# Norm weights applied ahead of the projections, the root behind them, in a two-layer hybrid block on one core

## The reference

```
h = rmsnorm(x, norm1_g);  P = h @ w_in            # four parts: rwkv, dsa, retention, gates
merged = sum over 3 branches of sigmoid(gate) * (y_branch @ w_branch)
x = x + merged @ w_o
h2 = rmsnorm(x, norm2_g)
x = x + square(relu(h2 @ w_up)) @ w_down          # d_ff = 4096
rmsnorm(x, g) = x * rsqrt(mean(x*x) + 1e-6) * g
```

## Time and profile before

| | |
|---|---|
| median of three runs | 2961.14 us (2960.81 to 2964.19) |
| profiled execution | 2957.23 us, of which 2955.4 us is the span of the profile |
| busy: PE, DVE, ACT, POOL | 91%, 44%, 19%, 35% of the span |

### The profile page before, as it was taken

One profiled execution on the slowest core, in us unless ns is written; L12 is line 12 of the kernel. 1 busy time (PEld: TensorE's weight loads), 2 busy tenths in 40 slices (PEclk: granted clock), 3 DMA queues, 4 the chain that ended last, 5 costly groups with the idle time before them and its releaser, 6 DMA issues.

```text
span 2955.4 us, 61291 instructions
## 1 busy us (share of the span) xinstructions
PE 2691.1 (91%) x24862; PEld 2460.6 (83%) x24862; DVE 1309.7 (44%) x2092; ACT 575.8 (19%) x1233; POOL 1032.4 (35%) x596
## 2 busy tenths in 40 slices
PE   7978899599998999999989789995999989999997
PEld 6877688389887989999988678874998789899997
DVE  3245885433337442332252468844343363522332
ACT  2112223411212120110111112233121211200111
POOL 3502232011223545555533033320222245455553
PEclk9979899699999999999999799986999999999999
DMA  4201112111133312222232111111111343222221
GB/s 169 87 28 62 42 58 71 57 46 48 51 120 116 122 59 85 85 79 84 85 106 73 36 58 47 61 64 46 58 51 54 120 135 98 65 86 79 84 85 53
DMA packets 64552, 222.53 MB, mean 75 GB/s; under 512 B 7888, under 2 KB 8656, under 8 KB 63056
## 3 DMA queue, kind: packets, MB, share of 16 engines
q1 hardware_dynamic: 43200, 158.23, 16.8%
q10 hardware_dynamic: 21136, 61.17, 5.9%
HBM read 190.34 MB, written 29.03 MB: 74 GB/s over the span
## 4 chain that ended last, share of the span: by engine, by line
PE 79%; DVE 10%; DVEq 5%; issue 3%; ACT 2%; ACTq 1%; DMA 0%
PE dense L460 62%; PE mix L460 15%; DVEq L1348 5%; ACT region_b L934 1%; DVE region_b L1528 1%; DVE region_b L1582 1%; PE mix L837 1%; DVE region_b L1584 1%; DVE region_a L1367 1%; DVE in_lo L1701 0%; DVE region_b L1641 0%; DVE region_b L1595 0%; DVE x L1563 0%; PE mix L535 0%; DMA x<-in_x 0%
## 5 line engine op out<-in xcount | busy, mean ns | idle before, releaser
L460 PE MATMUL dense<-act_hi,w_hi 128*128 128x288 f32 x3296 | 969.8, 309 | 40.0 <-DVE act_lo L1360 29.0
L444 POOL TENSOR_SCALAR w_hi<-w_raw 128x1024 fp32r<-128x1024 f32 x296 | 312.5, 1056 | 1865.6 <-PE dense L460 1502.8
L460 PE MATMUL dense<-act_lo,w_hi 128*128 128x288 f32 x3296 | 929.7, 297 | 0.0
L447 POOL TENSOR_TENSOR w_lo<-w_raw,w_hi 128x1024 fp32r<-128x1024 f32 x296 | 719.8, 2432 | 24.7
L460 PEld LDWEIGHTS dense<-act_hi,w_hi 128*128 128x128 f32 x3296 | 626.9, 190 | 103.8 <-issue 49.2
L460 PE MATMUL dense<-act_hi,w_lo 128*128 128x288 f32 x3296 | 707.3, 296 | 0.0
L460 PEld LDWEIGHTS dense<-act_lo,w_hi 128*128 128x128 f32 x3296 | 628.4, 191 | 0.0
L460 PEld LDWEIGHTS dense<-act_hi,w_lo 128*128 128x128 f32 x3296 | 534.5, 190 | 0.0
L460 PE MATMUL dense<-in_hi,w_hi 128*128 128x288 f32 x1408 | 399.0, 297 | 23.9 <-DVE y_mix L1710 12.6
L460 PE MATMUL dense<-in_lo,w_hi 128*128 128x288 f32 x1408 | 398.4, 298 | 0.0
L460 PE MATMUL dense<-in_hi,w_lo 128*128 128x288 f32 x1408 | 304.8, 298 | 0.0
(11 more groups left out here) (180 smaller groups left out, 2583.5 us busy)
## 6 DMA issues: line engine op xcount, KB each, us to landing
w_raw<-in_stream SPq DMA_DIRECT2D x296, 512.0 KB, 3.5
y_mix<-gate_scratch ACTq DMA_DIRECT2D x48, 288.0 KB, 2.8
gate_scratch<-region_b ACTq DMA_DIRECT2D x36, 288.0 KB, 2.1
x_scratch<-x ACTq DMA_DIRECT2D x2, 2304.0 KB, 8.9
y_scratch<-y_mix ACTq DMA_DIRECT2D x2, 2304.0 KB, 8.0
x<-x_scratch ACTq DMA_DIRECT2D x2, 2304.0 KB, 10.0
y_mix<-y_scratch ACTq DMA_DIRECT2D x2, 2304.0 KB, 9.5
gate_scratch<-region_a ACTq DMA_DIRECT2D x12, 288.0 KB, 2.1
```

What stands on the lines that cost most here:

```text
L444: nc.gpsimd.tensor_scalar(w_hi[:, v, :], w_raw[:, s, :], 1.0, 1.0, ALU.mult, ALU.mult).then_inc(w_high, 1)
L447: nc.gpsimd.tensor_tensor(w_lo[:, v, :], w_raw[:, s, :], w_hi[:, v, :].bitcast(F32), ALU.subtract).then_inc(w_split, 1)
L460: return nc.tensor.matmul(out, lhsT, rhs, start=start, stop=stop, skip_group_check=True)
```

## The change

The norm weight is taken into the operand at once, and the root is multiplied onto what leaves PSUM: `(x*g*r) @ W = ((x*g) @ W) * r`, with r per token.

- ACT squares a column tile and right behind it writes the high part of x times the weight; DVE writes the low part (`low_part`) and adds up the squares (`sum_square`). PE does the first tile behind a norm as its slices come, and only then the sum, of two products instead of eight (`sum_squares` stands behind tile 0).
- Behind w_in the root goes onto whatever reads PSUM: the rotary tables (multiplied by the root once a layer, two multiplications of 128 x 1152), v and gates of retention, dsa's v and index weights, the RWKV tiles (`shift_raws`, now on DVE, in the step in which the tile is finished, with ACT making mu times the row before), and the 24 gates as they come back from DRAM (`scale_gate`). In the MLP DVE does relu times root, ACT square and rounding.
- The roundings of the branch inputs and of the merged results go from DVE to ACT. x is loaded, and y stored, in 8 pieces.
- in_hi and in_lo grow from 12 to 16 tiles, so that MLP input and hidden tiles have places of their own. The first MLP chunk on PE and the last one on DVE are written out ahead of and behind the loop.

The diff, cut to its core:

```diff
             def sum_squares(n):
-                for k in range(KT):
-                    pe.wait_ge(sq_ready, n * KT + k + 1)
-                    wide(mix[0], ones, n_sq[:, k % 2, :], T, k == 0, k == KT - 1).then_inc(ssq_ready, 1)
+                pe.wait_ge(sq_summed, n * (KT - 2) + KT - 2)
+                wide(mix[0], ones, n_sum, T, True, False)
+                pe.wait_ge(sq_ready, n * KT + KT)
+                wide(mix[0], ones, n_sq[:, 1, :], T, False, True).then_inc(ssq_ready, 1)
...
+                    if t == 0:
+                        pe.wait_ge(in_const, 32)
+                        sum_squares(l * 2)
...
-                sum_squares(l * 2 + 1)
-                with pe.Fori(0, FF) as c:
+                def mlp_chunk(c, first=False):
                     for m in range(2 * KT):
                         up = m < KT
                         fresh = None
-                        if m == 0:
+                        if first and m == 0:
                             fresh = lambda k: pe.wait_ge(act_ready, l * (2 * KT) + (KT + k + 1))
                         if m == KT:
                             fresh = lambda k: pe.wait_ge(mlp_split, START + l * (FF * KT) + c * KT + k + 1)
                         dense_tile(m % SPLIT, m % 2, l * NT + T_MLP + c * (2 * KT) + m + 1,
-                                   free_before(U_MLP + m, l) + c * KT,
-                                   act_hi if up else in_hi, act_lo if up else in_lo, fresh=fresh)
-                sum_squares(l * 2 + 2)
+                                   free_before(U_MLP + m, l) + c * KT, in_hi, in_lo, k0=0 if up else KT, fresh=fresh)
+                        if first and m == 0:
+                            sum_squares(l * 2 + 1)
+                mlp_chunk(0, True)
+                with pe.Fori(1, FF) as c:
+                    mlp_chunk(c)
+            sum_squares(2 * DEPTH)
...
-            def squares(n, waits):
+            def squares(n, waits, high, gain, gains=None):
                 nc.scalar.preload_act_table_set(EXP_LN)
                 for k in range(KT):
                     waits(k)
                     if k >= 2:
-                        act.wait_ge(ssq_ready, n * KT + k - 1)
+                        act.wait_ge(sq_summed, n * (KT - 2) + max(1, k - 2))
                     op(n_sq[:, k % 2, :], x[:, k, :], ACT.Square).then_inc(sq_ready, 1)
+                    if k == 0 and gains is not None:
+                        act.wait_ge(in_par, gains)
+                    op(high[:, k, :], x[:, k, :], ACT.Copy, scale=pr(gain, k)).then_inc(high_ready, 1)
...
+                    if t >= 12:
+                        act.wait_ge(ret_gate, l * 4 + (t - 11))
+                        op(gate_sig(t - 12), rg[:, t - 12, :], ACT.Sigmoid).then_inc(ret_sig, 1)
...
-                        u = T_RW + f
-                        buf = taken(l, u, u)
-                        if f >= 2:
-                            act.wait_ge(shift_dve, l * N_RW + (f - 1))
-                        op(pt[:, f % 2, 1:HALF + 1], buf[:, 0, :], ACT.Copy)
-                        op(pt[:, f % 2, HALF + 1:TP + 1], buf[:, 1, 0:TP - HALF], ACT.Copy)
-                        op(pt[:, f % 2, TP + 1:TP + 2], pr("shift", f), ACT.Copy)
-                        op(shift_out[:, f:f + 15:14], buf[:, 1, TP - HALF - 1:HALF:C], ACT.Copy)
-                        op(pt[:, f % 2, TP + 2:TX + 1], buf[:, 1, TP - HALF:HALF], ACT.Copy).then_inc(shift_act, 1)
-                        act.wait_ge(shift_act, l * N_RW + (f + 1))
-                        act.sem_inc(dense_free[u % 2], 1)
+                        act.wait_ge(shift_raw, l * N_RW + (f + 1))
+                        if f:
+                            act.wait_ge(shift_dve, l * N_RW + f)
+                        op(d_t, pt[:, f % 2, 0:TX], ACT.Copy, scale=pr("mu", f)).then_inc(shift_mu, 1)
...
+                def merged_high(mp):
+                    for mi in range(2):
+                        act.wait_ge(br_merged, l * KT + (2 * mp + mi + 1))
+                        op(act_hi[:, 2 * mp + mi, :], merged[:, mi, :], ACT.Copy).then_inc(br_mhigh, 1)
                 for n in range(2):
                     load_gate(n)
                 for n in range(24):
                     if n + 2 < 24:
                         load_gate(n + 2)
-                    act.wait_ge(in_gate[n % 3], l * 128 + (16 * (n // 3) + 16))
+                    act.wait_ge(gate_scaled, l * 24 + (n + 1))
                     op(gate_in[:, n % 3, :], gate_in[:, n % 3, :], ACT.Sigmoid).then_inc(gate_ready, 1)
-                squares(l * 2 + 1, after_dve(l, U_WO))
+                    if n % 6 == 0 and n:
+                        merged_high(n // 6 - 1)
+                merged_high(3)
...
+            def sum_square(n, k):
+                if not 1 <= k <= KT - 2:
+                    return
+                dve.wait_ge(sq_ready, n * KT + (k + 1))
+                v.tensor_tensor(n_sum, n_sq[:, 0, :] if k == 1 else n_sum, n_sq[:, k % 2, :],
+                                ALU.add).then_inc(sq_summed, 1)
+                settle()
+            def low_part(n, k, hi, lo, gain):
+                dve.wait_ge(high_ready, n * KT + (k + 1))
+                v.scalar_tensor_tensor(lo[:, k, :], x[:, k, :], pr(gain, k), hi[:, k, :].bitcast(F32), ALU.mult,
+                                       ALU.subtract).then_inc(act_ready, 1)
+            def residual(l, n, m, t, buffer, hi, lo, gain):
+                if m:
+                    sum_square(n, m - 1)
+                    low_part(n, m - 1, hi, lo, gain)
+                dve.wait_ge(w_used, used_after(t, l))
+                v.tensor_tensor(halves(x[:, m, :]), halves(x[:, m, :]), out_of(dense[buffer]),
+                                ALU.add).then_inc(dense_free[buffer], 1)
+                if m == KT - 1:
                     settle()
-                for k in range(KT):
-                    if k >= 2:
-                        low(k - 2)
-                    v.scalar_tensor_tensor(n_t[:, k % 2, :], x[:, k, :], gain(k), n_rs, ALU.mult,
-                                           ALU.mult).then_inc(normed, 1)
-                low(KT - 2)
-                low(KT - 1)
+                    low_part(n, m, hi, lo, gain)
...
+                v.tensor_tensor(by_token(r_tab), by_token(r_tab), root_twice, ALU.mult)
+                v.tensor_scalar(mu_own[:, :], par[:, PARAMS["mu"][0]:PARAMS["mu"][0] + N_RW], -1.0, 1.0, ALU.mult, ALU.add)
...
+                def gated_ret(h):
                     dve.wait_ge(ret_sig, l * 4 + (h + 1))
-                    v.tensor_tensor(halves(rg[:, h, :]), out_of(dense[u % 2]), halves(rg[:, h, :]), ALU.mult).then_inc(dense_free[u % 2], 1)
+                    v.tensor_tensor(rg[:, h, :], rg[:, h, :], gate_sig(h), ALU.mult)
+                for t in range(8, N_RET):
+                    dve.wait_ge(w_used, used_after(T_RET + t, l))
+                    dst = rv[:, t - 8, :] if t < 12 else rg[:, t - 12, :]
+                    mm = v.tensor_tensor(halves(dst), out_of(dense[t % 2]), halves(n_rs), ALU.mult)
+                    mm.then_inc(dense_free[t % 2], 1)
+                    if t >= 12:
+                        dve.wait_ge(dense_free[t % 2], free_before(T_RET + t, l, 1))
+                        dve.sem_inc(ret_gate, 1)
+                    if t >= 13:
+                        gated_ret(t - 13)
+                gated_ret(3)
+                dve.wait_ge(in_tab, l * 16 + 16)
+                v.tensor_tensor(by_token(s_tab), by_token(s_tab), root_twice, ALU.mult)
...
+                def shift_raws(tiles):
                     for t in tiles:
                         if t >= N_RW:
                             continue
-                        cur = pt[:, t % 2, :]
-                        dve.wait_ge(shift_act, l * N_RW + (t + 1))
-                        v.tensor_tensor(d_t, cur[:, 0:TX], cur[:, 1:TX + 1], ALU.subtract)
-                        settle()
-                        v.scalar_tensor_tensor(shifted[t], d_t, pr("mu", t), cur[:, 1:TX + 1], ALU.mult,
+                        u, cur = T_RW + t, pt[:, t % 2, :]
+                        dve.wait_ge(w_used, used_after(u, l))
+                        if t >= 2:
+                            dve.wait_ge(shift_mu, l * N_RW + (t - 1))
+                        buf = out_of(dense[u % 2])
+                        v.tensor_copy(cur[:, TP + 1:TP + 2], pr("shift", t))
+                        v.tensor_tensor(cur[:, 1:HALF + 1], buf[:, 0, :], n_rs[:, 0:HALF], ALU.mult)
+                        v.tensor_tensor(cur[:, HALF + 1:TP + 1], buf[:, 1, 0:TP - HALF], n_rs[:, HALF:TP], ALU.mult)
+                        v.tensor_tensor(cur[:, TP + 2:TX + 1], buf[:, 1, TP - HALF:HALF], n_rs[:, TP:T],
+                                        ALU.mult).then_inc(shift_raw, 1)
+                        dve.wait_ge(shift_raw, l * N_RW + (t + 1))
+                        dve.sem_inc(dense_free[u % 2], 1)
+                        v.tensor_copy(shift_out[:, t:t + 15:14], cur[:, TP:TX + 1:TX - TP])
```

(54 more changed lines are left out.)

205 lines of the change are left out of this document (116 added, 89 removed).

## The result

The changed kernel takes 2993.52 us (median of 4 runs, 2991.46 to 2994.78) against 2960.97 (4 runs, 2960.16 to 2964.19) for the kernel before on the same chip: ratio 1.0114, 95% interval 1.0102 to 1.0127. It is slower, as forecast, but by 32.6 us where 16 were forecast. The profiled execution took 2993.07 us, its span is 2991.3; the span of before is 2955.4, so 35.9 us have to be found.

What follows compares the result with a forecast made beforehand. PE, busy 91% of the span, was taken as the bound, so time lies where it stands or does removable work. Gains of 76.8 us against a price of 92.8 gave +16, 2977 us; range 2906 to 2996.

Steps and rivals of the forecast that it cites:

- the branch entry: Entry to the branches, twice: DVE free some 5 us earlier as ACT rounds; -2.7 us each, -5.4, bounds 0 and -10.
- The holes in attention: RWKV tiles in attention, 14 a layer: PE waits while DVE meets tiles finished in the same step; +30.1 us a layer, +60.2.
- The clock of those holes: Attention: work lost at 1.2 GHz behind five holes of 3.3 us or more; 6 us a layer, +12, bounds 0 and 18.
- rival D: Every hole over 2 us brings 1.2 GHz, PE's jump costs 2.5, start gains only 10: +28, 2989 us; chance 0.10.
- The MLP: MLP: DVE's relu frees the buffer in place of ACT's; no cost, with 0.7 us of cover left, 8 times.
- The branches: Branch outputs, 24 half tiles, twice: PE waits for DVE at changes of group; +7.3 us a layer, +14, bounds 0 and 20.
- the row of 0.88: Profile row in the branch stage: a DVE addition beside POOL's TENSOR_SCALAR took 0.88 us, read against the split's first half holding DVE.
- Between the layers: Norm between the two layers: 27.4 us to the second tile becomes 8.5; -18.9 us.
- The start: Kernel start: tile 1 starts at 25 us in place of 38.5; -13.5 us, bounds -10 and -16.
- The norms: Norm behind w_o, twice: 22.8 us to the second MLP tile becomes 8.5; -14.3 us each, -28.6.
- the end: From the last MLP product to the span's end: 23.4 us becomes 13.0; -10.4 us.
- the retention entry: Ahead of retention, twice: PE waits longer for added DVE products and the dsa table; +3.3 us each, +6.6, bounds 3 and 8.

Runs made afterwards that it cites:

- e3: Changed kernel, but DVE empties a finished RWKV tile one attention step later, ACT and token shift following: 2903.05 us, ratio 0.9813.
- e9: Changed kernel with the multiplication of the probabilities by the reciprocal on ScalarE in place of VectorE: 2963.51 us, ratio 1.0017.
- e1: Changed kernel with 16 unused words ahead of region_a, so in_hi and in_lo start at a multiple of 128 bytes again: 2973.15 us, ratio 1.0044.
- e2: Kernel before with 16 unused words ahead of region_a, so in_hi and in_lo start 64 bytes behind a multiple of 128: 2964.56 us, ratio 1.0018.
- e10: Changed kernel with 24 unused words ahead of region_a, so in_hi and in_lo start 32 bytes behind a multiple of 128: 2985.0 us, ratio 1.0094.
- e5: Changed kernel with TensorE's loop over the two layers written out twice: 2987.57 us, ratio 1.0101.
- e8: Changed kernel with the dsa tables' multiplication behind the retention steps and the last retention gate's behind the fourth step: 2988.52 us, ratio 1.0106.
- e4: Kernel before with eight pauses of chosen length a layer put into PE's attention work: 3012.14 us (one run).
- e6: Changed kernel with the edits of e3 and e1 together: 2886.07 us, ratio 0.975.
- e7: Changed kernel with the edits of e3, e1, e5 and e8 together: 2880.32 us, ratio 0.9744.

## Why the prediction came out as it did

**The sign and the mechanism were right.** The gains were forecast as 76.8 us. Without the branch entry they were 71.4 against 64.9 measured. The holes in attention were forecast as 30.1 us a layer, tile by tile; measured 27.3, most within 0.5 us of their forecast (2.1, 1.2, 4.2 in the first block became 1.75, 1.0, 3.97). e3 shows that they hang on the wait for the step's own tile, e9 that POOL's split makes 2 us of the held ones.

**The step that failed is "The clock of those holes".** I counted five holes of 3.3 us or more, gave each a stretch like that behind w_o, some 3.5 us at 1.2 GHz, and took 6 us of lost work a layer, with 18 for both layers as the bound. Eight of ten holes were followed by 1.2 GHz, down to the one of 1.75 us, and three for 6.8 us. 37.6 us a layer at that level cost 17.2: +34.4 in place of +12, beyond the bound. It is rival D's mechanism ("every hole over 2 us brings the 1.2 GHz level"), at about twice its size of 9 us a layer. Two slips in the sum add to it: five holes at the 1.8 us of that row are 9 us a layer and not 6, and D's own rule meets eight of the listed holes, which is 14.4 and not 9. The one row I had the earlier trace rows averaged a single long hole over 22 us; it could not tell what a short hole costs, and in attention PE was never idle before. But the trace of the kernel before has short holes between its retention steps. Two of them, each with what follows it (columns as in the windows above):

```profile
159.36:161.35 1.99, 0.00 (x1) 0.03 (x1) 1.70 (x4) 0.60 (x1) 0.00 (x0) 1.00 0.00 0
162.06:165.47 3.41, 3.41 (x18) 3.41 (x17) 1.78 (x3) 0.60 (x1) 0.00 (x0) 0.50 0.00 0
...
189.07:191.06 1.99, 0.00 (x0) 0.03 (x1) 1.70 (x4) 0.60 (x1) 0.00 (x0) 1.00 0.00 0
191.06:196.00 4.94, 4.94 (x44) 4.77 (x44) 1.98 (x3) 0.60 (x1) 0.00 (x0) 1.00 0.02 3
```

The same hole, 1.99 us, brought 3.4 us at 1.2 GHz once and none the other time. Read ahead of the forecast, these rows would have taken the limit of 3.3 us out of it.

**The MLP was given nothing, and cost 11.1.** The term looked at buffers and at who frees them; that was right, there is no hole. It did not look at where the operands lie. That `mu_own` moves everything behind it by 64 bytes and that the up half would read the moved tensor are both in the diff, and e1, e2 and e10 show that the shift is the cause, though not in full how it acts.

**The branches went the other way:** -5.5 in place of +8.6. PE's waits in the changed kernel's stage from 938 us to w_o's end (engine, line: us, times, longest), against 6.6 and 5.6 us on the same two lines before:

```profile
PE dense L489 <- DVE y_mix L1824: 4.9, 4, 1.7
PE dense L489 <- DVE in_lo L1793: 4.4, 1, 4.4
```

At a change of group PE waits 1.0 to 1.7 us, where 2.2 was worked out, and at the entry the second wait, 6.3 us long before, is 1.15, where 2.7 was taken off in all. As to POOL, the prediction misread the row of 0.88. That addition began 0.36 us ahead of POOL's second half, so only the last 0.28 us of the first half lay beside it. The timeline of DVE and POOL in the changed kernel's MLP shows the subtraction L1844 beside either half:

```profile
1134.13 1.06 POOL L473 TENSOR_SCALAR w_hi<-w_raw 128x1024 fp32r<-128x1024 f32 x1 [2.52 <-issue]
1134.96 0.83 DVE L1844 TENSOR_TENSOR in_lo<-y_mix,in_hi 128x576 fp32r<-128x576 f32 x1 [0.23 <-DVE y_mix L1851]
1135.27 2.77 POOL L476 TENSOR_TENSOR w_lo<-w_raw,w_hi 128x1024 fp32r<-128x1024 f32 x1
...
1136.39 2.26 DVE L1844 TENSOR_TENSOR in_lo<-y_mix,in_hi 128x576 fp32r<-128x576 f32 x1 [0.60 <-ACT in_hi L972]
```

It took 0.83 us 56 times, begun with 0.2 us of the first half left, and 2.26 us 8 times, begun with 1.65 us of the second half left, where the same operation alone took 0.76 before. In all 64 cases it ended 0.6 us after the half that ran when it began. So both halves hold it alike, as the page of the Trainium skill named in the prediction (SBUF — State Buffer, Who interferes with whom) has it, and the price is what is left of the half; an operation that reads PSUM (L1824, 0.76 beside either) is free. That the branches came out cheaper than forecast is therefore no sign that the first half holds nothing.

**Smaller terms.** Between the layers -14.6 in place of -18.9: the jump, given 0 with 2.5 as its bound, was 3.26 and 1.5 for the clock behind it. The start missed by 2.0, the chain has 2.1 and 2.8 us in DVE's queue at the first two tiles, which the sum did not have. The norms, the end and the retention entry were right within 0.5 us. The misses in the branches (14 us too dear) and in the clock and the MLP (22 and 11 too cheap) partly cancel; a sum that lies within its range says little on its terms.

## What to carry to other kernels

Where an engine's list is in program order, an operation that waits for what another engine finishes in this very step belongs behind everything that this other engine is about to need; one step of delay here was worth 90 us of 2993. Price a hole in a busy TensorE stretch by the clock as well as by its length, and look for short holes of the same length in the trace that you already have; an experiment with pauses of known lengths costs one run. And read a diff for what it does to addresses: a 56-byte tensor declared ahead of the matmuls' operands cost 20 us in the median, more than the start or the end gained.

## What was not expected of the hardware

- The pace of six matmuls of 128x288 goes with the start address of the moving operand: 0.807 us 64 bytes behind a multiple of 128 (all MLPs of the changed kernel, e3, e5, e8 and e9, and the down half of e2), 0.800 at 32 bytes, and at a multiple mostly 0.780 to 0.790, but 0.800 in the second layer of before and of e4 (down half) and 0.807 in that of e6 and e7, in one execution each. Matmuls on an operand that stayed in place changed with the same shift, from 43.75 to 44.31 us for 336 (43.75 in all layers but one without it, 44.31 in all with it).
- A hole in PE's work in these stretches brought 0, 3.4, 6.8 or 10.2 us at 1.2 GHz, and length alone does not tell which: two holes of 1.99 us in the kernel before, with the same work in them, brought 3.4 us and none, one of 3.97 brought 3.4 and one of 3.24 brought 6.8. None of 1.6 us or less in attention brought any.
- A TENSOR_SCALAR, or a TENSOR_TENSOR with both inputs in SBUF, that VectorE begins while POOL works on its split ends only behind POOL's instruction: 0.15 us behind it at 256 columns (2.38 us where 0.35 is the operation's own time), 0.6 us behind it for a TENSOR_TENSOR of 576 columns, beside POOL's first half and its second alike. ScalarE's multiplication took 0.51 beside it.
- PE's jump back to the head of a long loop showed as 3.3 us of kind issue, and with the loop written out the two layers met without a hole.
